# Layer 1's norms: first sums as eight accumulating products with ones, in place of a running total

## What is computed

```python
def layer_norm(x, g, b):
    mu = x.mean(-1, keepdims=True)
    var = jnp.square(x - mu).mean(-1, keepdims=True)
    return (x - mu) * lax.rsqrt(var + LN_EPS) * g + b

x = layer_norm(ALPHA * x + mix, ln1_g, ln1_b)      # mix ends in "@ w_out"
x = layer_norm(ALPHA * x + squared_relu_mlp(x, w_ff1, w_ff2), ln2_g, ln2_b)
```

## Time and profile before

| | us |
|---|---|
| median of 3 runs | 4060.24 (4058.21 to 4060.54) |
| the profiled execution, its own time | 4059.24 |
| its span, first to last instruction | 4057.2 |
| TensorE busy, share of span | 3594.9, 89% |
| VectorE busy | 1872.4, 46% |
| ScalarE busy | 1132.4, 28% |
| GpSimd busy | 694.7, 17% |
| mean granted TensorE clock | 0.929 of 2.4 GHz |

### The profile page before, as it was taken

How to read it: one execution, slowest core, us unless ns; L and a number is a source line. 1 busy time by engine, 2 the same in 40 slices (tenths; PEclk the granted TensorE clock), 3 DMA queues, 4 the chain that set the end, 5 groups by cost and what they waited for, 6 DMA issues and landing times.

```text
span 4057.2 us, 38900 instructions
## 1 busy us (share of the span) xinstructions
PE 3594.9 (89%) x16574; PEld 2904.9 (72%) x16574; DVE 1872.4 (46%) x1809; ACT 1132.4 (28%) x1477; POOL 694.7 (17%) x287
## 2 busy tenths in 40 slices
PE   8888697999999777888788999999969899999797
PEld 6555375888888477655568899989857777777576
DVE  4444545222222668655436556446563323444323
ACT  3333233111111432333533111111132423322232
POOL 2111032222222211100001122212111111111042
PEclk9888798999999888888889999999989999999699
DMA  3000031111111210000011111111121111000132
GB/s 111 21 21 21 16 109 57 47 48 50 48 47 47 69 53 32 26 6 0 6 58 40 45 46 44 47 47 47 42 78 42 47 63 47 27 32 27 43 127 100
DMA packets 55892, 191.14 MB, mean 47 GB/s; under 512 B 6804, under 2 KB 7188, under 8 KB 55208
## 3 DMA queue, kind: packets, MB, share of 16 engines
q1 hardware_dynamic: 55720, 188.66, 13.6%
HBM read 171.78 MB, written 16.86 MB: 46 GB/s over the span
## 4 chain that ended last, share of the span: by engine, by line
PE 73%; DVE 17%; ACT 7%; issue 2%; DMA 1%; SPq 0%; DVEq 0%; ACTq 0%
PE psum L263 20%; PE psum L265 19%; PE psum L264 19%; PE psum L136 13%; DVE mix L105 3%; DVE res L96 2%; DVE work L96 2%; DVE res L105 2%; ACT work L124 1%; ACT w_hi L129 1%; DVE x_lo L96 1%; DVE x_lo L105 1%; DVE softmax_columns L111 1%; PE psum L134 1%; ACT L124 1%
## 5 line engine op out<-in xcount | busy, mean ns | idle before, releaser
L263 PE MATMUL psum<-x_hi,w_hi 128*128 128x512 f32 (+2 forms) x3472 | 1316.9, 379 | 100.1 <-DVE x_lo L96 32.9
L264 PE MATMUL psum<-x_lo,w_hi 128*128 128x512 f32 (+2 forms) x3472 | 1265.4, 364 | 0.0
L96 POOL TENSOR_TENSOR w_lo<-w_raw,w_hi 128x1024 fp32r<-128x1024 f32 x283 | 694.5, 2455 | 3327.1 <-ACT w_hi L129 3327.0
L265 PE MATMUL psum<-x_hi,w_lo 128*128 128x512 f32 (+2 forms) x3472 | 1262.4, 364 | 0.0
L263 PEld LDWEIGHTS psum<-x_hi,w_hi 128*128 128x128 f32 x3472 | 664.7, 191 | 222.8 <-issue 55.1
L129 ACT CAST w_hi<-w_raw 128x1024 fp32r<-128x1024 f32 x283 | 296.5, 1048 | 1660.1 <-PE psum L265 1653.3
L264 PEld LDWEIGHTS psum<-x_lo,w_hi 128*128 128x128 f32 x3472 | 665.7, 192 | 98.2 <-issue 20.3
L265 PEld LDWEIGHTS psum<-x_hi,w_lo 128*128 128x128 f32 x3472 | 662.4, 191 | 85.8
L263 PE MATMUL psum<-h_hi,w_hi 128*128 128x512 f32 x864 | 347.5, 402 | 36.7 <-DVE res L96 11.2
L265 PE MATMUL psum<-h_hi,w_lo 128*128 128x512 f32 x864 | 344.7, 399 | 0.0
L264 PE MATMUL psum<-h_lo,w_hi 128*128 128x512 f32 x864 | 342.7, 397 | 0.0
(11 more groups left out here) (243 smaller groups left out, 3589.8 us busy)
## 6 DMA issues: line engine op xcount, KB each, us to landing
w_raw<-w_dram SPq DMA_DIRECT2D x283, 512.0 KB, 3.2
res<-spill SPq DMA_DIRECT2D x4, 1044.0 KB, 8.8
res<-x_dram SPq DMA_DIRECT2D x8, 512.0 KB, 8.8
res<-x_dram SPq DMA_DIRECT2D x4, 1024.0 KB, 8.0
spill<-res SPq DMA_DIRECT2D x1, 4096.0 KB, 12.1
spill_a<-mix SPq DMA_DIRECT2D x8, 512.0 KB, 2.6
res<-spill_a SPq DMA_DIRECT2D x4, 1024.0 KB, 8.1
x_plain<-spill SPq DMA_DIRECT2D x4, 1024.0 KB, 8.6
```

The lines of the kernel that those rows point to most:

```text
L96: self.mark(self.e.tensor_tensor(out, a, b, op), inc)
L263: t.e.matmul(out, whi, xhi, start=k == 0, stop=False, skip_group_check=True)
L264: t.e.matmul(out, whi, xlo, start=False, stop=False, skip_group_check=True)
L265: ins = t.e.matmul(out, wlo, xhi, start=False, stop=last_k, skip_group_check=True)
```

## The change

The running total on VectorE and its buffer go. Instead, each chunk of `res` is multiplied by ones as soon as it is evicted, and the eight products accumulate in the bank of the first sum. A new `pe_row` issues one of them and waits for the eviction of its product (`p.freed`). Row m - 1 is issued after product m; the last one, row 7, stands where the sum was. The last row (c = 7) signals ScalarE. The shared `pe_sum` counts four totals fewer.

```diff
@@ HalfNorm
     def pe_sum(self, t, u, total):
         i = u % 2
-        t.wait_ge(self.total, u + 1)
+        t.wait_ge(self.total, u - 3)
         t.wait_ge(self.k.ones_set, 1)
         t.mm([(self.k.ps[:, 4 + i, :], self.k.ones[:, :], total, True, True)], self.summed)
+
+    def pe_row(self, t, u, c, x, p):
+
+        t.wait_ge(*p.freed)
+        product = (self.k.ps[:, 4 + u % 2, :], self.k.ones[:, :], x, c == 0, c == 7)
+        if c == 7:
+            t.mm([product], self.summed)
+        else:
+            out, ones, rows, start, stop = product
+            t.e.matmul(out, ones, rows, start=start, stop=stop, skip_group_check=True)
@@ Ffn1
-                self.total = core.sbuf("total_1", [P, S], ctx=inner)
...
@@ pe_out, after each product m
+            if m:
+                self.pe_row(t, i, m - 1, ("out1", i, m - 1))
+
+    def pe_row(self, t, u, m, key):
+        i = u % 2
+        self.norm.pe_row(t, u, m, self.k.real(m)[:, 512 * i:512 * i + 512], self.k.products[key])
@@ pe_project, after each product m
+            if m and half is not None:
+                self.pe_row(t, 2 + half, m - 1, ("ff2", g, m - 1, half))
@@ pe_norm
-        self.norm.pe_sum(t, u, self.total[:, 512 * i:512 * i + 512])
+        self.pe_row(t, u, 7, ("out1", i, 7) if u < 2 else ("ff2", 7, 7, i))
@@ dve_products, "out1" and the halves of "ff2"
-                self.dve_total(v, i, m)
...
-                    self.dve_total(v, half, m)
-
-    def dve_total(self, v, i, m):
-
-        if m:
-            cols = slice(512 * i, 512 * i + 512)
-            v.settle()
-            v.tt(self.total[:, cols], self.k.real(0)[:, cols] if m == 1 else self.total[:, cols], self.k.real(m)[:, cols], ALU.add,
-                 inc=self.norm.total if m == 7 else None)
```

## The result

| | before | after |
|---|---|---|
| median on one chip, 20 runs each, us | 4060.41 (4057.05 to 4064.48) | 4067.28 (4063.15 to 4069.80) |
| the profiled execution, its own time | 4059.24 | 4067.58 |
| its span | 4057.2 | 4065.5 |
| TensorE busy | 3594.9 | 3623.4 |
| VectorE busy | 1872.4 | 1847.6 |

The ratio is 1.0015 (95% interval 1.0008 to 1.0022): 6.9 us slower by the medians, and still within the 0.2% (8.1 us) that the prediction called no change, though the interval's upper end lies just above it. The prediction was 4063.9, in a range of 4056.4 to 4073.5.

The account below looks back on a forecast made before the run. TensorE carries 73% of the chain of waits, VectorE 17%. Terms 4.4 + 4.4 - 1.5 - 1.0 - 2.6 = +3.7 us on 4059.24 give 4062.9, stated as a 4063.9 median; range 4056.4 to 4073.5, own range 4060 to 4068.3.

Parts of the forecast that it names:

- likeliest case: Whole kernel: no change that can be told, within 0.2% (8.1 us); chance 0.74.
- H2: Norm 2's first half: same pattern as norm 1's first half, rows between gapless weight products, same 1.50 us wait; +4.4 us.
- H3's squares: Eight bare squares after norm 2's second half: TensorE arrives from work, so the clock is up; -2.6 us, or 0.
- H1: Norm 1's second half: three old waits go, new ones come, TensorE's work 58.1 us; net -1.5 us.
- H3: Norm 2's second half: rows 2 to 4 held by evictions, fifth eviction earlier, part at slow clock; net -1.0 us.
- Price of a product with ones: TensorE, each row between weight products: 0.86 us at full clock, 24.1 us more work for 28 of them.
- rival of 0.46: Each product with ones costs only 0.46 us, the distance between records; total 4056.4 us, chance 0.04.
- H0: Norm 1's first half: rows 0 to 5 cost 5.16 us, row 6 free, row 7 wins 0.72; net +4.4 us.
- slow clock: Rival: norm 2's second half stays at 1.2 GHz from row 4 on, squares gain nothing; 4073.8 us, chance 0.17.
- three new waits: Norm 1's second half: TensorE held by evictions at the third, fourth and fifth rows, 2.0 us together.
- bound of -3.5: Norm 1's second half: best case, no new wait, or VectorE 2 us earlier per stretched total; -3.5 us.
- All slack real: Rival: norm 1's second half -3.5, norm 2's second half -2.8, bare squares -2.6; 4060.1 us, chance 0.19.

Follow-up runs that it names:

- doubled: The changed kernel with rows 0 to 6 of both norms' first halves issued twice, the second into an unread bank; 4074.07 us, ratio 1.0032 to the kernel before.
- norm 2 alone: Rows of ones only in norm 2, while norm 1 keeps the running totals of the kernel before; 4062.49 us, ratio 1.0005 to the kernel before.
- late rows' kernel: Changed kernel, but first halves total chunks 0 to 6 on VectorE with one row for chunk 7, and norm 2's second half lags three products; 4042.16 us.
- lag 3: The changed kernel, but in norm 2's second half row m follows product m+3 instead of m+1; 4056.17 us, ratio 0.9992 to the kernel before.
- first halves' kernel: Rows of ones only in both norms' first halves, second halves keep the kernel before's running total; 4072.26 us, ratio 1.0029 to the kernel before.
- second halves alone: Rows of ones only in both norms' second halves, first halves keep the kernel before's running total; 4052.20 us, ratio 0.9981 to the kernel before.

## Why the prediction was right or wrong

- **The median**: 4063.9 forecast, 4067.28 measured, inside the forecast's own range of 4060 to 4068.3 (whose edges are not what the bounds named for it add up to), and no more than 0.2%. The likeliest case came as a time. Behind it stand two misses of the same direction, H2 (+2.9) and H3's squares (+2.6), and two of the other, H1 (-0.5) and H2's squares with H3 (-1.5). That they leave 3.4 us in the median is partly luck.
- **Price of a product with ones, 0.86 us**: right, 0.86 between evictions when doubled. The rival of 0.46 has fallen.
- **H0, +4.4**: right, +4.40 measured, row 6 free and the 0.72 us won included.
- **H2, +4.4**: this is the term of the sum that was mis-sized. It measured +7.27 and +7.22, of which 4.4 are the rows (norm 2 alone: 4.56) and 2.8 are matmuls at 1.2 GHz behind waits that both kernels have. "Same pattern" took the clock of before for granted, although norm 1's step shifts everything in this place. Its rival, slow clock, was looked for in H3 alone.
- **H1, -1.5**: -1.95 measured. That the square's wait of 2.02 us and GpSimd's 1.59 go was right. Two errors met here: of three new waits of 2.0 us together one came, with 0.46, and TensorE's own work was 1.1 us more than the 58.1 added up. The bound of -3.5, in which VectorE gains 2 us for a stretched total, did not come; in its place the scale at 592.04 took 2.78 us. That the 0.69 us credited for each total is the right size was not measured.
- **H3, -1.0**: by itself +0.04, with H2's squares -2.46. Expected were 0.6 us from the total ahead of the last centrings; H2's squares gained 2.50. So row 4 starts 3.5 us earlier against the steps ahead of it, not 2.0. From there to row 7 the 9.93 us are those forecast, 9.9; the clock was down for part of the way, as charged (0.83 on average over this stretch), and the waits at rows 2 to 4 came to 12.8 us together against 12 predicted.
- **H3's squares, -2.6**: wrong, +0.02, and this is the prediction's own sign that it is wrong, or within 0.2 us of it (8.83 where it named 9). The reason given, that TensorE arrives from 10 us of work and so at full clock, holds for the arrival (rows 6 and 7 start at 1413.61 and 1414.55, 0.94 us apart) but not for what follows: VectorE's first centring fell on GpSimd's subtraction at 1415.05, the first square waited 2.98 us instead of 2.15, and the clock went down. The window after, against 0.87 in the earlier trace rows for 1413 to 1420:

```profile
1409.00:1413.00 4.00, 4.00 (x17) 2.91 (x16) 0.69 (x1) 0.00 (x0) 0.00 (x0) 1.00 0.00 0
...
1416.00:1422.00 6.00, 3.34 (x4) 1.32 (x5) 5.59 (x8) 2.78 (x5) 1.39 (x1) 0.74 0.58 193
```

  Where the centrings start behind GpSimd's subtraction, as in the late rows' kernel (it ends at 1393.31, they start at 1393.92), the 2.5 us are there. That the subtraction makes the difference is read from the timelines and was not tried by itself. From H2's squares to H3's together -3.6 were predicted and -2.4 measured: the error of the squares is more than half made up by that of the term before it, which is luck.
- **The rivals**: slow clock in H3 did not come. It asked for more than about 7 us at half clock from row 4 on; TensorE was at 1.00 for 1397 to 1405 and again from 1409, and a mean of 0.83 over the 9.93 us makes about 3.4 us at half. Its other half, squares that gain nothing, did come. All slack real fell with H2 and with H3's squares.
- **What wasn't seen** is the rule of one product's lag itself. The prediction named the three waits of 12 us and took them for nearly free, since an eviction sets the end. With lag 3 they give 10 us: the worth of work that could be done during these waits was in the sum (8.1 us behind row 4) and was not set against another order.

## What to carry to other kernels

Moving sums from VectorE to TensorE pays only in the stretches where TensorE waits for VectorE's backlog; ask it for each stretch, and mix both ways, since here the halves gave +12.5 and -7.6 us and the mix -18. A side product that is tied to a late eviction undoes the run-ahead that banks gave, so let it lag by more than one product (3 with four banks gave 11 us in H3; no lag between was tried). And VectorE's relief is worth what stands next to GpSimd at that moment: one total of 0.69 us more or less decided 2.5 us in one place and 1.4 in another.

## What the runs showed of the hardware that was not expected

The clock's answer to a wait depends on more than the wait. The same wait for the same square, with the same 12 us of work ahead of it to 0.01 us, left TensorE at 2.4 GHz in the kernel before and took it down to 1.2 in the first halves' kernel (granted clock of the next 4 us 1.00 and 0.67). The effect is reproducible for one program: two profiles of the change agree within 0.05 us in H2. Two readings are not told apart here: that it moves with a shift of a few microseconds, or that it depends on work further back, since ahead of these 12 us the first halves' kernel has H0's rows. It was worth 2.8 us in H2 of the change, and most of the 4.4 us that the first halves' kernel lost outside its rows. What sets it remains open.

The parts add up less well than their sum looks. By medians first and second halves alone give +12.5 - 7.6 = +4.9 us and the whole +6.9, which the intervals do not tell apart; the steps of the profiles add to +7.2 and +7.5. But H2 alone is 4.9 in the parts and 7.3 in the whole, and H0's squares +0.2 and -1.4: the single steps differ by more than their sums.
